# A hybrid decoder step: the decay subtraction gated by two output pieces, clamp and exponentials as two steps, softplus in two parts, tables kept by ScalarE, the end rearranged

## The reference

```python
proj = rmsnorm(x, norm_mix) @ w_in      # z, xbc, dt, sc_b, sc_c, sc_h, gate_a, gate_b
xs, B, C = split(silu(causal_dwconv(xbc)))              # 4 taps
dt = softplus(dt_raw + bias);  A = -exp(a_log);  Acum = cumsum(dt * A) per chunk of 128
W = (C @ B.T) * exp(where(causal, Acum_l - Acum_s, -inf)) * dt
y = W @ xs + (C @ h_prev) * exp(Acum) + D * xs          # 64 heads in 8 groups; states returned
branch_a = (groupwise_rmsnorm(y * silu(z))) @ w_ssm_out
branch_b = (sc_b * causal_dwconv(sc_c * sc_h)) @ w_sc_out
x = x + (sigmoid(gate_a) * branch_a + sigmoid(gate_b) * branch_b) @ w_o
x = x + (silu(causal_dwconv(n2 @ w_gate)) * (n2 @ w_up)) @ w_down,   n2 = rmsnorm(x)
x = x + (pe @ w_ple) * sigmoid(rmsnorm(x) @ w_ple_gate);   y_out = rmsnorm(x, norm_final)
```

## Time and profile before

| | us |
|---|---|
| median of 3 runs (lowest, highest) | 2935.49 (2932.91, 2936.19) |
| profiled execution | 2937.35 |
| its span | 2935.6 |
| PE busy | 2879.9 (98%) |
| DVE, ACT, POOL busy | 1738.7, 1180.6, 280.8 |
| PE's granted clock, mean | 0.994 |

### The profile page before, as it was taken

The page is one execution under the profiler, slowest core; times in us unless marked ns, Lnnn a source line. Parts: engine busy times, 40 slices in busy tenths (PEclk is TensorE's granted clock), DMA queues, the critical chain, the costliest instruction groups (busy, mean ns, idle before and its releaser), DMA issues.

```text
span 2935.6 us, 53200 instructions
## 1 busy us (share of the span) xinstructions
PE 2879.9 (98%) x20040; PEld 2807.6 (96%) x20040; DVE 1738.7 (59%) x2169; ACT 1180.6 (40%) x1738; POOL 280.8 (10%) x448
## 2 busy tenths in 40 slices
PE   7999999999999999999999999999999999999997
PEld 6899999999999999999999999999999999999997
DVE  7676866767677655555555555755555555555564
ACT  4443544445444433333333333533333333333443
POOL 2211211212112100000000000100000000000101
PEclk9999999999999999999999999999999999999999
DMA  7565665656646565555555555555555555555463
GB/s 200 143 180 156 167 185 146 182 144 178 182 141 194 144 187 158 144 148 152 148 145 152 153 147 153 141 147 148 153 149 151 143 154 147 149 151 148 138 175 108
DMA packets 753279, 457.32 MB, mean 156 GB/s; under 512 B 14633, under 2 KB 747233, under 8 KB 752625
## 3 DMA queue, kind: packets, MB, share of 16 engines
q1 hardware_dynamic: 679065, 411.59, 49.6%
q10 hardware_dynamic: 73464, 42.01, 5.1%
q0 software_dynamic: 672, 2.66, 0.2%
HBM read 430.73 MB, written 25.47 MB: 155 GB/s over the span
## 4 chain that ended last, share of the span: by engine, by line
PE 91%; DVE 4%; ACT 2%; issue 2%; POOL 0%; DMA 0%; ACTq 0%; DVEq 0%; SPq 0%; POOLq 0%
PE ps L1558 28%; PE ps L1559 28%; PE ps L1560 28%; PE ps L1751 1%; PE ps L1742 1%; PE ps L1911 1%; DVE cv L1117 1%; PE ps L1929 1%; ACT wm L888 1%; DVE wlo L997 1%; ACT wm L884 0%; PE ps L1925 0%; DVE acc_a L1278 0%; ACT whi L661 0%; PE ps L1772 0%
## 5 line engine op out<-in xcount | busy, mean ns | idle before, releaser
L1558 PE MATMUL ps<-n_hi,whi 128*128 128x320 f32 x4144 | 1289.8, 311 | 10.7 <-DVE wlo L997 7.8
L1559 PE MATMUL ps<-n_lo,whi 128*128 128x320 f32 x4144 | 1283.5, 310 | 0.0
L1560 PE MATMUL ps<-n_hi,wlo 128*128 128x320 f32 x4144 | 1283.1, 310 | 0.0
L997 DVE TENSOR_TENSOR wlo<-raw,whi 128x1024 fp32r<-128x1024 f32 x746 | 921.2, 1245 | 505.3 <-ACT whi L661 504.8
L661 ACT ACTIVATE whi<-raw 128x1024 fp32r<-128x1024 f32 x746 | 783.5, 1057 | 898.3 <-PE ps L1560 840.6
L1558 PEld LDWEIGHTS ps<-n_hi,whi 128*128 128x128 f32 x4144 | 780.0, 188 | 14.1 <-DVE wlo L997 8.1
L1559 PEld LDWEIGHTS ps<-n_lo,whi 128*128 128x128 f32 x4144 | 780.1, 188 | 0.6
L1560 PEld LDWEIGHTS ps<-n_hi,wlo 128*128 128x128 f32 x4144 | 779.8, 188 | 0.0
L1558 PE MATMUL ps<-c_hi,whi 128*128 128x320 f32 x1728 | 537.3, 311 | 14.5 <-DVE acc_a L1278 14.0
L1560 PE MATMUL ps<-c_hi,wlo 128*128 128x320 f32 x1728 | 535.2, 310 | 0.0
L1559 PE MATMUL ps<-c_lo,whi 128*128 128x320 f32 x1728 | 535.0, 310 | 0.0
(11 more groups left out here) (288 smaller groups left out, 1814.6 us busy)
## 6 DMA issues: line engine op xcount, KB each, us to landing
raw<-in_w_in SPq DMA_DIRECT2D x322, 512.0 KB, 5.2
raw<-in_w_ffn_gate SPq DMA_DIRECT2D x88, 512.0 KB, 4.3
raw<-in_w_ffn_up SPq DMA_DIRECT2D x88, 512.0 KB, 5.1
raw<-in_w_ffn_down SPq DMA_DIRECT2D x88, 512.0 KB, 4.1
raw<-in_w_ssm_out SPq DMA_DIRECT2D x64, 512.0 KB, 4.3
h<-in_state_ssm ACTq DMA_DIRECT2D x32, 512.0 KB, 4.9
out_ssm_sample<-hn ACTq DMA_DIRECT2D x32, 512.0 KB, 4.7
raw<-in_w_sc_out SPq DMA_DIRECT2D x32, 512.0 KB, 4.2
```

What stands on the lines that cost most here:

```text
L997: tt(wlo[slot][:], raw[slot][:], whi[slot][:].bitcast(F32), SUB).then_inc(lo_split, 1)
L1558: mm(out, w_h, x_h, start=first, stop=False)
L1559: mm(out, w_h, x_l, start=False, stop=False)
L1560: return mm(out, w_l, x_h, start=False, stop=last)
```

## The change

- `decay` on POOL waits, in the loop, until `out_added` has reached 8g - 6, the second out piece of the round. `clamp` and `exps` are now steps of their own: clamp right after decay, exps after the sixth out piece; in group 0 decay comes before x5, clamp after it, exps after z0.
- `dtstart` (after x0) and `dtend` (after x1) hold the two parts of softplus; in group 0 `bc` comes after x4 instead of before it.
- The tables' transposes stand inside the norm, before the last quarter, in four banks; ACT copies them. The `dcol` copies move before DVE's last n_lo.
- At the end PE adds the last squares itself in a second PSUM pass, three of four tiles are transposed earlier, both engines scale all three row blocks, and SP issues the stores.

```diff
-        head = x(1, 2) + [("dturn", 0)] + x(3) + [("dtab", 0), ("bc", 0)] + x(4, 5)
-        tail = [("unit", "z", 0), ("decay", 0), ("ssd1", 0), ("unit", "z", 1), ("mask", 0)]
+        head = (x(1) + [("dtend", 0)] + x(2) + [("dturn", 0)] + x(3) + [("dtab", 0)] + x(4)
+                + [("bc", 0), ("decay", 0)] + x(5) + [("clamp", 0)])
+        tail = [("unit", "z", 0), ("exps", 0), ("ssd1", 0), ("unit", "z", 1), ("mask", 0)]
     else:
-        head = (x(0, 1) + [("norm", 0)] + x(2, 3) + [("bc", 0)] + x(4) + OUT8[:5] + [("decay", 0)] + OUT8[5:]
-                + [("mask", 0)] + x(5))
+        head = (x(0, 1) + [("norm", 0)] + x(2, 3) + [("bc", 0)] + x(4) + OUT8[:5] + [("decay", 0), ("clamp", 0)]
+                + OUT8[5:6] + [("exps", 0)] + OUT8[6:] + [("mask", 0)] + x(5))
...
-    Seg("prologue", 0, 0, 1, [("start", 0), ("unit", "dt", 0), ("unit", "x", 0)]),
+    Seg("prologue", 0, 0, 1, [("start", 0), ("unit", "dt", 0), ("unit", "x", 0), ("dtstart", 0)]),
...
+            for c in range(3):
+                rows = P if c < 2 else NS
+                sp.wait_ge(y_scaled_a, c + 1)
+                sp.wait_ge(y_scaled_v, c + 1)
+                sp.dma_start(dst, yrow[c][0:rows, :]).then_inc(y_stored, 16)
...
                     if h < 3:
                         first_split(h + 1)
+                    if h == 2:
+                        for n, (dst, bank, col, width) in enumerate(TAB_COPIES):
+                            act.wait_ge(tab_turned, n + 1 if n < 3 else len(TAB_COPIES))
+                            activate(dst, ps[:, bank, col:col + width], copy).then_inc(tab_kept, 1)
...
+                    act.wait_ge(y_gained, 3 * (KM // 4 - 1))
+                    for c in range(3):
+                        rows = P if c < 2 else NS
+                        part = yrow[c][0:rows, 0:Y_SPLIT]          # Y_SPLIT = 1024
+                        activate(part, part, copy, scale=rms_t[0:rows, c:c + 1]).then_inc(y_scaled_a, 1)
...
+                        part = yrow[c][0:rows, Y_SPLIT:DM - 512]
+                        ts(part, part, scale, None, MUL)
...
                     pool.wait_ge(acum_loaded, 32 * (g + 1))
+                    if seg.start:
+                        pool.wait_ge(out_added, 8 * g - 6)
...
-                elif kind == "unit" and step[1] == "pg" and j % 2:
+                elif kind == "unit" and step[1] == "pg" and j % 2 and not (j == 3 and seg.start == KM // 4 - 1):
...
                 low(1)
+                if seg.name == "prologue":
+                    turn_tables()
                 high(3)
...
+            def last_sums(part, first):
+                for c in range(3):
+                    rows = P if c < 2 else NS
+                    for t in range(2):
+                        last = mm(ps[0:rows, c, 0:1], part[:, t, token_rows(c)], ones[:, 0:1],
+                                  start=first and t == 0, stop=not first and t == 1)
+                return last
...
-                    turn_rows(KM // 4)
-                    pe.wait_ge(sq_added, ADDED[4] + 9)
+                    pe.wait_ge(y_gained, 3 * (KM // 4 - 1))
+                    turn_rows(KM // 4, range(3))
+                    pe.wait_ge(sq_added, ADDED[4] + 8)
+                    last_sums(sq_sum, True)
+                    turn_rows(KM // 4, range(3, 4))
+                    pe.wait_ge(sq_ready, SQUARES[4] + 8)
+                    last_sums(sq_pair[1], False).then_inc(sq_summed, 1)
```

More of the change, by code:

```diff
@@ L310, in hybrid_decoder @@
         xst, sst = xstate[:].rearrange(flat3), sstate[:].rearrange(flat3)
[L311 to L315, removed]
+        TAB_COPIES = [(ptab[:, 0:512], 2, 0, 512), (xst[:, 0:512], 3, 0, 512), (xst[:, 512:1024], 4, 0, 512),
+                      (xst[:, 1024:1152], 5, 0, 128), (sst[:, 0:256], 5, 128, 256),
+                      (ptab[:, 512:N_PARAMS], 5, 384, N_PARAMS - 512)]
+        TAB_SOURCES = [[(prow[:, b, :], P) for b in range(4)],
                        [(xsrow[:, b, :], P) for b in range(4)], [(xsrow[:, b, :], P) for b in range(4, 8)],
[L317 removed]
+                       [(xsrow[:, 8, :], P)], [(ssrow[:, b, :], P) for b in range(2)],
+                       [(prow[0:N_PARAMS - 512, 4, :], N_PARAMS - 512)]]
         N_PARAM_LOADS = 2 + sum(1 for row, rows in PARAMS.values() for b in range(PARAM_BLOCKS)
@@ L826, in tasks @@
                     rms(seg, it, j)
-                elif kind == "unit" and step[1] == "dt":
+                elif kind == "dtstart":
                     act.wait_ge(dt_min, 1)
@@ L878, in tasks @@
                     activate(bt[0:NS, 2, :], ps[0:NS, 5, 2 * P:3 * P], copy).then_inc(bt_kept, 1)
-                elif kind == "decay":
+                elif kind == "clamp":
                     for c in range(3):
@@ L1104, in start @@
                 lower(2)
+                dve.wait_ge(cols_loaded, 16 * 3)
+                for half in range(2):
+                    v.tensor_copy(dcol[half * HD:half * HD + HD, :],
+                                  drow[half * HD:half * HD + HD, :].rearrange("p (q two) -> p two q", two=2)[:, half, :])
                 lower(3)
@@ L1146, in keep, with dt_parts @@
                               ps[0:NS, bank, 2 * HEADS:3 * HEADS].rearrange("p (g h) -> p g h", g=GROUPS))
+            def dt_parts():
+                return [wm[0:HEADS, i, 0:NT] for i in range(5)]
             def tasks(seg, it, step, pos, outs_end):
@@ L1155, in tasks @@
                 elif kind == "unit" and step[1] == "dt":
[L1158 to L1167, removed]
+                    pass
+                elif kind == "dtstart":
+                    w = dt_parts()
+                    dve.wait_ge(multiplied, unit_end(seg, it, 0))
                     dve.wait_ge(x_saved, 16 * 4)
@@ L1645, in unit, with turn_tables @@
                     last.then_inc(multiplied, 1)
+            def turn_tables():
+                pe.wait_ge(params_loaded, 16 * N_PARAM_LOADS)
+                pe.wait_ge(x_kept_v, KM // 2)
+                pe.wait_ge(x_kept_a, KM // 2)
+                for (_, bank, col, _), sources in zip(TAB_COPIES, TAB_SOURCES):
+                    for src, rows in sources:
+                        last = turn(ps[:, bank, col:col + rows], src, ident[0:rows, 0:rows])
+                        col += rows
+                    last.then_inc(tab_turned, 1)
             def units_of_norm(seg, it, n):
@@ L1694, in add_squares, with turn_rows @@
                     last.then_inc(sq_summed, 1)
-            def turn_rows(it):
-                pe.wait_ge(ple_added, 4 * it)
+            def turn_rows(it, tiles_of=range(4)):
+                pe.wait_ge(ple_added, 4 * it - 3 + tiles_of[-1])
                 for c in range(3):
                     rows = P if c < 2 else NS
-                    for m in range(4):
+                    for m in tiles_of:
                         last = turn(ps[0:rows, 4 + c, m * P:(m + 1) * P], final[:, m, token_rows(c)], ident[:])
-                    last.then_inc(y_turned, 1)
+                    if m == 3:
+                        last.then_inc(y_turned, 1)
+            def last_sums(part, first):
[5 more added lines that the diff above has]
+                return last
             def turn_inputs(j):
@@ L1787, in tasks @@
                         units_of_norm(seg, it, {"prologue": 1, "ffn": 2, "ple": 3}[seg.name])
[L1788 to L1795, removed]
                 elif kind == "out":
```

29 lines of the change are left out of this document (8 added, 21 removed).

## The result

| | before | after |
|---|---|---|
| median (lowest to highest), us | 2935.84 (2932.91 to 2938.14), 4 runs | 2908.10 (2907.59 to 2910.22), 4 runs |
| span of the profiled execution | 2935.6 | 2906.6 |
| PE's granted clock, mean | 0.994 | 0.997 |

The ratio is 0.9911 (95% interval 0.9899 to 0.9923): 27.7 us faster, where 30.5 had been forecast. The profile of the kernel before is of one of its longer executions (2937.35): of 28 further runs of it, taken beside the experiments, one took 6467 us and is left out, and the other 27 have a median of 2934.0, against which the change gains 25.9 us.

The account below looks back on a forecast made before the run. PE is busy 98%, so only its idle time, lower-rate time, head and tail can give: 19.1 + 10.0 + 1.6 = 30.7 us off 2937.35 gives 2906.7, less 1.9 to the median 2904.8, written 2905; range 2898 to 2917.

Parts of the forecast that it names:

- Part 1: Seven loop rounds: GpSimd's subtraction moved off x4's taps, behind the second out add, removes PE's waits; 3.9 + 11.8 us.
- Rivals B: Loop: a held split or add still stops PE once a round, the subtraction's gain is lost; 2920.5 us, chance 0.09.
- C: Loop: each subtraction stops DVE, adds included, and PE loses 7.0 us a round; slower, 2954 us, chance 0.03.
- rival D: Loop: second add long over before POOL gets there, so the wait does nothing; 2920.5 us, chance 0.02.
- A: Prologue gives nothing: the wait at dturn and the lower rate eat its gain; 2914.8 us, chance 0.17.
- E: Prologue: no lower rate anywhere and dt 2 us earlier, so more gain; 2898.9 us, chance 0.07.
- Part 2: Seven loop rounds: clamp and exponentials apart on ACT, with a split between, remove PE's 0.49 us a round; 3.4 us.
- Part 3: Prologue and first pair: softplus 3.4, dtab and bc 2.7, x5 -0.6, pair 0 4.9, tables -0.4; 10.0 us, bounds 3 to 14.
- The bc order: Prologue: x4 between dtab and bc removes the heads_tab wait, perhaps the lower rate; 1.0 to 4.3 us, taken as 2.7.
- softplus in two parts: Prologue: second half of unit x1 no longer waits, dturn waits 4.7 us instead; 3.4 us gained, bounds 1 to 5.5.
- The idle time at the tables: Prologue: PE idles about 2.4 us after the tables' transposes; net 0, bounds 0.5 gained to 1.6 lost at the lower rate.
- Part 4: End: PE sums the last squares, rows scaled in thirds, first store earlier; 1.6 us gained, bounds 0.5 to 2.5.

Follow-up runs that it names:

- e2: Kernel before, with only GpSimd's wait for the second output piece added: 2921.93 us.
- e1: Changed kernel without GpSimd's wait for the second output piece, clamp and exponentials still apart: 2923.33 us.
- e3: Changed kernel with clamp and exponentials in one block again after the fifth out piece, in the loop: 2911.24 us.
- e8: Changed kernel with bc of group 0 before unit x4 again, decay left in its new place: 2909.12 us.
- e11: Changed kernel with decay, clamp and exponentials of group 0 back in one block behind unit z0: 2913.51 us.
- e5: Changed kernel with softplus undivided again, after the taps of x0 and before x1: 2907.73 us.
- e6: Changed kernel with the old end (last add on POOL, 1536 columns on ACT, stores on ACT's queue): 2908.54 us.
- e7: Changed kernel with PE's transposes of dt moved between the two halves of unit x3: 2903.05 us.
- e10: Changed kernel with PE's dt transposes between the halves of unit x3 and the subtraction waiting for x4's taps instead of the second out add: 2903.60 us.
- e9: Changed kernel with GpSimd's subtraction waiting for the fourth out add of the round instead of the second: 2910.14 us.

## Why the prediction was right, point by point

- **Part 1, the subtraction: right, in cause and size.** 15.7 us predicted; e2 gained 15.7 in its loop, e1 lost 14.7 there and 15.2 in all. The layout holds too: a first split that runs its 1.23 us while POOL waits, an add, and a second split held, due 4.7 us after the third piece's start in both. Its add, due at 7.0 us, was done at 8.0 where I had 8.6.
- **The rule on the shared port agrees with these traces.** The add, with one input in PSUM, ran in 0.82 us in the middle of a subtraction, the split, with both in SBUF, in 2.40 us. The Trainium skill, SBUF — State Buffer, section Who interferes with whom, says both, and its section SBUF: two separate sides adds that whoever starts first has the pair for the whole instruction; the split of 1.23 us, beside which POOL's first operation took 2.95 us instead of 1.89, agrees. Rivals B (the lock moves to the outs, 2920.5) and C (2954) fail because no add was held and no wait for `acc_a` is left, rival D (the wait does nothing) by e1, A (the prologue gives nothing, 2914.8) by the 9.0 us of the next point but one, and E by the lower clock behind `dturn`.
- **Part 2, ACT's block in two: right.** 3.4 predicted, 3.1 in the total by e3 and 4.0 in its loop.
- **Part 3, the prologue and group 0: 10.0 predicted, 9.0 measured between the marks, 8.2 with the later start.** Up to `dturn` 4.7 us came where 5.0 were forecast. Between `dturn` and `dtab` the term was mis-sized: the lower clock behind the 4.4 us wait cost 2.8 us and not 1.6. From `dtab` to the first norm 7.1 us came for a forecast of 7.0, but by another division, and with luck in it. The bc order gave 1.0 (e8) where I had 2.7: the old order came back and the lower clock did not. The place of decay gave 5.9 in the traces and 5.4 in the totals (e11) where I had 4.3 (4.9 less 0.6 for a held operation at the transposes of `xs`, where PE waited 1.2 us for `xs`, against 0.3 before and 2.6 and 2.7 in e2 and e11). Taken against e2, which has the old order of both and neither lower stretch, the change from `dtab` to the first norm is 3.6 us (87.1 to 83.5) and not 7.1. So what this part is worth depends on which execution of the old order is laid beside it, and I had read its prices from one.
- **A step that was right in sum and wrong as a reason: softplus in two parts.** I had credited the division with freeing x1. e5 shows that the division frees nothing; the stall is 4.4 us in one place or 5.0 in the other. What freed x1 is that softplus stands behind the unit x0 and its splits, divided or not, and that the table copies are off DVE; dt itself starts 4.9 us later than before.
- **The idle time at the tables.** 1.97 us with no lower clock behind it in the changed kernel's profile; the first loop round of before had 2.09 us and then 1.4 us lost. The bound of 1.6 us for it was a fair one: in e1, with the same code and the same 1.97 us, the lower clock came and cost 1.5 us.
- **Part 4, the end: right.** 1.6 in the trace, both ways (17.6 to 16.0, and back in e6). The first store itself comes 2.0 us sooner (7.9 to 5.9), so 0.4 of it is not seen at the end.
- **The rest.** The terms give 30.7, the spans 29.0. The difference is 1.0 in part 3 and 0.8 by the later first load, over which the change has no say: e8's transposes started at 6.3 and e7's at 6.8, with the same code up to there. The forecast of 2904.8 lies 3.3 us under the measured 2908.1: these 1.7 us, and 1.6 because the profiled execution of before lay 1.9 us above the median that I started from, while that of the changed kernel lies 0.2 above its own.

## What to carry to other kernels

Ask of each GpSimd operation which VectorE instructions with two SBUF inputs it meets, and let it start where those have some slack: here a wait of one line moved 5.6 us of GpSimd work by some 7 us, two output pieces, and gave half of the whole gain, and it could stand behind the taps as well, or two adds later at a price of 2 us. When an engine's long serial chain (softplus) stalls another, dividing the chain only chooses where the stall stands; moving the consumer behind more of its own work (e7, 5.0 us for one call moved) takes it away. Credit a stretch at the lower clock to an order of steps only when the old order, put back, brings it back, and in more than one profile: in e8 and e2 the wait of 1.0 us for `heads_tab` was there and the lower clock was not.

## What the runs showed of the hardware

- Whether the clock falls behind a short wait of PE is told neither by the length of the wait nor by the code. After the same 1.97 us (`n_hi`) it fell in e1 (0.50 in 44 to 46) and stayed at 1.00 in the changed kernel and the nine other experiments with that prologue; after 1.0 us for `heads_tab` it fell in the kernel before and not in e2 or e8; after 0.8 us for dt it fell in e7 and not in e10; after 2.6 us for `xs` it fell in e2 (0.57 in 108 to 112), and after 2.7 us in e11 it did not. Behind the waits of 4.3 to 5.0 us for dt's chain, and of 7.8 us in e2 and the kernel before, it fell each time. The runs don't settle what decides the short ones.
- The lower level costs in bursts: behind one wait of 4.4 us `dturn` to `dtab` took 10.5 us against 7.7.
- When DVE's instruction is first, GpSimd pays: the three subtractions took 4.76 us where no DVE instruction held them (group 0 of the changed kernel), 5.80 where one split did (e9), 6.79 where two did, and 5.61 beside the taps of x4, which they held in turn.
- The same code from the transposes of x to `dturn` took 58.9 to 60.1 us in seven profiles (the changed kernel's 59.5 among them) and 61.4 in the eighth (e1). An effect of 1 us is to be read in its own stretch and not in the total. Of the 61.4, 1.5 us are the lower clock behind `n_hi`.
